# Token rows of 1024 columns with their halo tokens apart, V weights loaded behind the first freed block, and a first tile taken block by block, in an encoder block on eight cores

## The reference, cut to what matters

```python
p = x @ w_in                     # columns: [B_A | C_A | H_A | U_B | V_B | GATE_A | GATE_B]
gates = sigmoid(p[..., OFF_GA:] + b_gate)
a  = b_a * conv3_centred(c_a * h_a, conv_w)               # width 1536, depthwise over tokens
bb = gelu(u_b) * (W_s LN(gelu(v_b)) + b_s)                # per chunk of 128 tokens, 8 heads
mix = (g_a * (a @ w_pa) + g_b * (bb @ w_pb)) @ w_o
x1 = layernorm(ALPHA * x + mix, ln1_g, ln1_b)
out = layernorm(ALPHA * x1 + square(relu(x1 @ w_ff1)) @ w_ff2, ln2_g, ln2_b)
```

## Time and profile before

| | us |
|---|---|
| median of 3 runs | 1142.12 (1141.73 to 1142.21) |
| the profiled execution | 1143.57 |
| its span (slowest core, core 6) | 1141.9 |
| spans of all cores | 1135.9 to 1141.9 |
| PE busy | 1119.3 (98%) |
| DVE busy | 523.7 (46%) |
| ACT busy | 266.6 (23%) |
| POOL busy | 141.0 (12%) |

### The profile page before, as it was taken

One profiled execution on the slowest core, in us unless ns is written; L12 is line 12 of the kernel. 1 busy time (PEld: TensorE's weight loads), 2 busy tenths in 40 slices (PEclk: granted clock), 3 DMA queues, 4 the chain that ended last, 5 costly groups with the idle time before them and its releaser, 6 DMA issues.

```text
span 1141.9 us, 15721 instructions; the slowest of 8 cores (1135.9 to 1141.9 us)
## 1 busy us (share of the span) xinstructions
PE 1119.3 (98%) x5582; PEld 546.4 (48%) x5690; DVE 523.7 (46%) x750; ACT 266.6 (23%) x439; POOL 141.0 (12%) x257
## 2 busy tenths in 40 slices
PE   7989999999999999999999999999999999999997
PEld 3445555444444444444455555554444444444444
DVE  1835465322248434512467545642222763442356
ACT  1224323111114333100012343221111343330000
POOL 4302200000011010200120121000000101000000
PEclk9999999999999999999999999999999999999999
DMA  9986676355556674674367439555443717444412
GB/s 142 164 152 130 131 135 121 58 82 84 93 91 97 107 115 79 111 123 74 74 115 143 102 98 185 98 94 83 69 64 53 121 38 127 79 80 81 78 56 92
DMA packets 48219, 114.71 MB, mean 100 GB/s; under 512 B 20496, under 2 KB 20880, under 8 KB 47632
## 3 DMA queue, kind: packets, MB, share of 16 engines
q0 software_dynamic: 25056, 88.23, 47.9%
q1 hardware_dynamic: 23088, 25.48, 8.1%
HBM read 189.33 MB, written 8.39 MB: 173 GB/s over the span
## 4 chain that ended last, share of the span: by engine, by line
PE 93%; DMA 4%; POOL 1%; issue 1%; DVE 0%; ACT 0%; DVEq 0%; POOLq 0%; ACTq 0%
PE ps L264 93%; DMA ring<-wblk 2%; DMA regR<-xT 2%; POOL t L585 0%; POOL regR L150 0%; POOL ring L150 0%; ACT t L502 0%; DVE regQ L911 0%; DVE regQ L916 0%; DVE regQ L583 0%; DVEq L1007 0%; DVE st L930 0%; DVE regQ L928 0%; DVE st L932 0%; DVE t L588 0%
## 5 line engine op out<-in xcount | busy, mean ns | idle before, releaser
L264 PE MATMUL ps<-regR,ring 128*128 128x512 bf16 (+1 forms) x3267 | 651.1, 355 | 10.6 <-DMA regR<-xT 4.2
L264 PEld LDWEIGHTS ps<-regR,ring 128*128 128x128 bf16 x3328 | 318.9, 98 | 325.6 <-issue 15.1
L264 PE MATMUL ps<-ring,regP 128*128 128x512 bf16 (+1 forms) x1035 | 220.5, 372 | 1.5 <-DMA ring<-wblk 0.4
L150 POOL DMA_DIRECT2D ring<-wblk x144 | 77.1, 540 | 701.5 <-PE ps L264 696.7
L264 PEld LDWEIGHTS ps<-ring,regP 128*128 128x128 bf16 x1056 | 103.3, 98 | 118.7 <-issue 0.9
L264 PE MATMUL ps<-regP,ring 128*128 128x512 bf16 x628 | 143.1, 379 | 0.6
L878 DVE TENSOR_TENSOR regP<-t 128x512 bf16<-128x512 f32 x128 | 87.7, 692 | 116.5 <-ACT t L877 116.5
L755 DVE TENSOR_TENSOR t<-ps,t 128x512 f32<-128x512 f32 x64 | 44.1, 691 | 180.3 <-ACT t L753 180.0
L877 ACT ACTIVATE t<-ps 128x512 f32<-128x512 f32 x128 | 75.9, 597 | 136.0 <-PE ps L264 128.1
L264 PEld LDWEIGHTS ps<-regP,ring 128*128 128x128 bf16 x640 | 62.6, 98 | 75.5
L753 ACT ACTIVATE t<-ps,colv 128x512 f32<-128x512 f32 x64 | 43.8, 687 | 189.7 <-PE ps L264 189.7
(11 more groups left out here) (67 smaller groups left out, 483.9 us busy)
## 6 DMA issues: line engine op xcount, KB each, us to landing
ring<-wblk POOLq DMA_DIRECT2D x128, 512.0 KB, 7.6
bigW<-wbig POOLq DMA_DIRECT2D x4, 2048.0 KB, 21.8
regQ<-x SPq DMA_DIRECT2D x16, 512.0 KB, 5.6
y<-regQ SPq DMA_DIRECT2D x15, 512.0 KB, 2.6
ring<-wblk POOLq DMA_DIRECT2D x16, 384.0 KB, 8.7
regR<-xT POOLq DMA_DIRECT2D x16, 256.5 KB, 14.2
ring<-wfirst POOLq DMA_DIRECT2D x6, 256.0 KB, 16.0
t<-ln1g SPq DMA_DIRECT2D x2, 512.0 KB, 6.7
```

Of the source, the lines that this page charges most:

```text
L150: self.items.append(lambda e, out=out, in_=in_, sem=sem: e.dma_start(out=out, in_=in_, transpose=transpose).then_inc(sem, 16))
L264: return lambda e: e.matmul(out, lhsT=l, rhs=r, start=st, stop=sp_)
```

## The change

Three things are changed.

1. The token rows in HBM have 1024 columns instead of 1026. The halo tokens of both super-tiles come in a tensor of their own, `xhT` (128 x 32 float32, 16 columns for each super-tile), which SP loads once into `xhf` in the prologue. `place_halo` copies and casts a super-tile's 16 values per partition into columns 1024 and 1025 of `xT` on ACT: for the first super-tile in the prologue, for the second at the start of F2. A buffer record `xhB` makes the groups that read the halo wait for the copy.
2. `load_big(0)` and the load of `wsTb` leave the prologue for `load_v()`, called right behind `release(0)` in `first_groups`: on POOL they stand behind the issue of block 8 and ahead of those of blocks 9, 11 and 12.
3. In F2, the first tile of the part that goes tile by tile makes one group per block, instead of one group over all its blocks. This holds for every half; with lb = 7 it is seven groups.

```diff
-            DMA(pool, xT[:, k0:k0 + n, 0:TH], xT_d[r0:r0 + n * 128, :].rearrange("(p k) n -> p k n", k=n), xT_sem[c], writes=wr)
+            DMA(pool, xT[:, k0:k0 + n, 0:T], xT_d[r0:r0 + n * 128, :].rearrange("(p k) n -> p k n", k=n), xT_sem[c], writes=wr)
+
+        def place_halo(st):
+            OP(act, lambda e: e.activation(out=xT[:, :, T:TH], in_=xhf[:, st * 16:(st + 1) * 16].rearrange("p (k n) -> p k n", k=8), func=AF.Copy),
+               reads=[xhfB], writes=[xhB])
...
+            DMA(sp, xhf[:], xh_d, sem_xh, writes=[xhfB])
             DMA(sp, colv[:], cv_d, sem_cv, writes=[colvB])
+            place_halo(0)
...
             OP(pool, lambda e: e.memset(chalf[:, 1:2], LN_EPS), writes=[memB])
+
+        def load_v():
             load_big(0)
             DMA(pool, wsTb[:], wsT_d.rearrange("p (h i) -> p h i", h=8), sem_ws, writes=[wsTbB])
...
-                    PEG(fns, reads=deps_ + w0B[1] + xTB, writes=[bankB[gi], bankB[bx]])
+                    PEG(fns, reads=deps_ + w0B[1] + xTB + [xhB], writes=[bankB[gi], bankB[bx]])
...
                     for i in (0, 1, 3, 4):
                         release(i)
+                        if i == 0:
+                            load_v()
...
             if not last:
                 for c in range(len(PIECES)):
                     load_xT(st + 1, c)
+                place_halo(st + 1)
...
                 for tt in range(7 if split else 8):
-                    f2_part(st, h, tt, list(range(8 - lb, 8)))
+                    for qs in [[q] for q in range(8 - lb, 8)] if tt == 0 else [list(range(8 - lb, 8))]:
+                        f2_part(st, h, tt, qs)
                     f2_drain(tt, h, None, split)
...
-            rows.append(_pieces(np.concatenate([xpad[g0 + 1:g0 + T + 2], xpad[g0:g0 + 1]], axis=0).T, PIECES))
+            rows.append(_pieces(xpad[g0 + 1:g0 + T + 1].T, PIECES))
+            halos.append(np.stack([xpad[g0 + T + 1], xpad[g0]], axis=1).reshape(8, 128, 2).transpose(1, 0, 2).reshape(128, 16))
```

More of the change, by code:

```diff
@@ L155, in build_program @@
     x_d = nc.dram_tensor("x", [TOK, D], F32, kind="ExternalInput").ap()
-    xT_d = nc.dram_tensor("xT", [ST * 1024, TH], F32, kind="ExternalInput").ap()
+    xh_d = nc.dram_tensor("xhT", [128, ST * 16], F32, kind="ExternalInput").ap()
+    xT_d = nc.dram_tensor("xT", [ST * 1024, T], F32, kind="ExternalInput").ap()
     w0_d = nc.dram_tensor("wfirst", [2 * 1024, 512], F32, kind="ExternalInput").ap()
@@ L189, in build_program @@
         ones = sb("ones", [128, 128], F32)
+        xhf = sb("xhf", [128, ST * 16], F32)
         hy = sb("hy", [128, 4, 4], F32)
@@ L361, in build_program @@
         colvB = Buf(accum=True)
+        xhfB = Buf(accum=True)
+        xhB = Buf()
         wsTbB = Buf(accum=True)
@@ L367, in build_program @@
         bigW_sem = [semaphore("bigw"), 0]
+        sem_xh = [semaphore("ld_xh"), 0]
         sem_ws = [semaphore("ld_ws"), 0]
@@ L600, in first_groups @@
                 if n < 2:
-                    PEG(weave(fns, halos(n, 2 + n)), reads=[WBB] + w0B[0] + xTB, writes=[bankB[bbk], bankB[2 + n]])
+                    PEG(weave(fns, halos(n, 2 + n)), reads=[WBB, xhB] + w0B[0] + xTB, writes=[bankB[bbk], bankB[2 + n]])
                     halo_out(n, 2 + n, hcs[n])
@@ L663, in stage_A @@
                         PEG([mm(ps[:, b, 0:third], (LO if kc < 4 else HI)[:, kc % 4, cols], xT[:, kc, ts_], kc == 0, kc == 7) for kc in range(8)],
-                            reads=[LOB, HIB] + xTB, writes=[bankB[b]])
+                            reads=[LOB, HIB, xhB] + xTB, writes=[bankB[b]])
                     if j == 1 and i == 2:
@@ L1058, in _host_layout @@
         rows = []
+        halos = []
         for st in range(ST):
             g0 = c * TOK + st * T
-            rows.append(_pieces(np.concatenate([xpad[g0 + 1:g0 + T + 2], xpad[g0:g0 + 1]], axis=0).T, PIECES))
-        per_core.append((xc, np.concatenate(rows, axis=0)))
+            rows.append(_pieces(xpad[g0 + 1:g0 + T + 1].T, PIECES))
+            halos.append(np.stack([xpad[g0 + T + 1], xpad[g0]], axis=1).reshape(8, 128, 2).transpose(1, 0, 2).reshape(128, 16))
+        per_core.append((xc, np.concatenate(rows, axis=0), np.ascontiguousarray(np.concatenate(halos, axis=1))))
     return cvs, wsT, bsrow, per_core
@@ L1097 @@
         m["xT"] = per_core[c][1]
+        m["xhT"] = per_core[c][2]
         in_maps.append(m)
```

## The result

The changed kernel takes 1147.48 us (median of six runs) beside 1141.99 us before: ratio 1.0047, 95% interval 1.0035 to 1.0060. By the ratio it is slower by about 5.4 us, where -0.7 us was forecast; the time lies outside the stated range.

A forecast was written before the change was run, and what follows sets the result against it. TensorE bounds 93% of the span with untouched matmuls; only the DMA-full first 85 us and single waits could move. Core 5's 1139.3 + 3.0 - 0.8 - 1.8, plus 1.7 around the span, gave 1141.4 us, range 1138.8 to 1144.0.

The forecast's parts named there:

- The wait for block 8 goes, and one for block 10 takes its place at ca=6, behind a hole in the queue: Near 65 us PE's wait vanishes; near 84 us a weight-block wait of 2 to 3.5 us appears.
- The hole, 3.1 us on core 3 and 4.3 on core 5: DMA queue empty between the last prologue block's landing and block 8's: 3.1 us lost on core 3, 4.3 on core 5.
- All behind it later by the hole: Block 10 lands 3.1 us later on core 3 (87.3); PE's new waits are 2.2 and, on core 5, 3.45 us.
- The clock falls at the new wait: Rival at ca=6: price 1.5 us; 1142.9 with the rows' gain (chance 0.10), 1144.7 without (0.12).
- Token rows, -1.8: First set's eight token loads: rows of 1024 columns save half of 3.6 us, 1.8; second set worth nothing.
- Last half block by block, -0.8 on the slowest core: Wait in front of 1082.84 us for the last half's seventh block goes: -0.8 us on core 5, 0 on core 3.
- The sum for the slowest core: Core 5: 1139.3 + 3.0 - 0.8 = 1141.5, less 1.8 for the token rows gives 1139.7 us.

The follow-up runs named there:

- wsT late: Changed kernel with the wsT load issued behind block 10 instead of right behind the V weights: 1.0030 of before, 1144.94 us.
- a quarter of V: Changed kernel with two of eight channel blocks of the V weights loaded in the prologue, the rest and wsT behind block 8: 1.0008 of before.
- half did: Changed kernel with the first 1 MB of the V weights loaded in the prologue, the rest and wsT behind block 8: 0.9971 of before.
- the 28 matmuls: Changed kernel with 28 matmuls of 512 columns, result never read, put in front of ca=6: 1.0034 of before, 1145.86 us.

## Why the prediction was wrong

- **The wait for block 8 goes, and one for block 10 takes its place at ca=6, behind a hole in the queue.** Right, and the direction of the V edit with it: later on cores 3 and 5. The kernel with V moved alone shows that this edit costs 7.7 us.
- **The hole, 3.1 us on core 3 and 4.3 on core 5.** This is the step that failed. It put the end of the queue's work at the landing of the last prologue block. But most of the DMA engines were through earlier. On core 6 that block landed at 44.97 (12.1 + 32.9), while the DMA share was already 0.17 from 42 us on; a block's load has 16 records of 4 bytes near its end (block 8's lie between 51.7 and 53.1 us), and of the last 16 before the hole 13 lie between 41.2 and 42.0 us and three at 43.2, 43.4 and 44.4. The idle time is 4.3 to 6.9 us. The same reading made the queue full "to 84 us" in the kernel before: its share on core 3 is 0.60 and 0.32 ahead of block 10's landing at 84.2.

```profile
78.00:82.00 4.00, 4.00 (x23) 2.10 (x22) 2.07 (x4) 1.93 (x4) 1.01 (x3) 1.00 0.60 102
82.00:86.00 4.00, 4.00 (x21) 1.81 (x19) 3.75 (x4) 2.15 (x2) 1.14 (x2) 1.00 0.32 48
```

- **All behind it later by the hole.** It was more. Counted from the landing of the last prologue block, block 10 came 4.2 to 9.4 us later than on the same core before. Between the landings of blocks 8 and 10 stand the same bytes on every core, and they took 33.0 to 37.5 us. And block 8 itself took 5.0 to 5.2 us on four cores, as the late blocks of core 3 did, but 6.9 to 7.7 on the other four, among them the three that end last. Late blocks didn't stand for this place; why is open (last section). So the new wait is 6.5 to 7.6 us on the slowest three cores instead of 2.2 to 3.45. On core 5, whose 3.45 us the sum rests on, it was 3.56, and that is luck: 6.7 us idle instead of 4.3, made up by the bytes behind block 8, which took 33.0 us there. Cores 0, 2 and 6 had no such luck, and the forecast worked out the new wait for cores 3 and 5 alone and gave core 6 that of core 3.
- **The clock falls at the new wait.** The sum had it at nothing, though the 3.45 us of core 5 are more than the 2.98 at which core 6 had lost its clock; it was a rival, at 0.22 with and without the rows' gain. It fell on five of eight cores, at waits of 3.65 to 7.58 us, and held at 2.85, 3.41 and 3.56 us. The size of the wait alone doesn't settle it: with wsT late it fell at 3.54 us, with a quarter of V at 2.27 on core 5 and not at 2.24 on core 7, and core 6 before lost it at 2.98. The price was 1.5 us on core 6, as forecast, and up to 2.7 on core 2. The rival's times of 1142.9 and 1144.7 were too low because they took the forecast's wait.
- **Token rows, -1.8.** The number came out, -1.8 us alone, but by luck. Half of the second set's difference was taken, on the ground that the destination's step stays. With the destination unchanged the second set's step fell by 0.35 us on the mean of the cores, and on core 3 from 2.03 to 1.51, where weights take 1.58: the whole difference went, and the ground was wrong. The first set gained only 0.2 us per load (its eighth load lands at 27.6 instead of 29.2 us on the mean of the cores), and why less than the second is not shown.
- **Last half block by block, -0.8 on the slowest core.** The wait goes as said; with a wait on some cores alone the times don't resolve it. With V in the prologue it is at most the difference of 0.9984 and 0.9976, whose intervals overlap.
- **The sum for the slowest core.** Forecast, core 5 at 1139.7; measured, core 6 at 1146.0, which is 1105.2 + 31.63 + 7.58 + 1.5 by the table. Of the 6.3 us between them 4.1 are the wait (7.58 instead of 3.45) and 1.5 the clock; the rest is the start of the long row, 31.63 where core 5's 32.72 less 1.8 gives 30.9.

## What to carry to other kernels

A load that looks like an obstacle in a queue may be what fills it while the next one can't be issued yet. Before moving it, find what stands in the queue in its place, and take the end of the work from the DMA share, not from a landing; then move only as much as leaves the queue full (here half did; that it beats moving nothing is not shown). And when a wait is replaced by another, price the new one with the loads that surround it, and add what a fallen clock costs.

## What the hardware showed that was not expected

- **Rows of 2048 bytes instead of 2052 in SBUF (4096 instead of 4104 in HBM)** lower a load's step from 1.97 to 1.62 us, 18%, for 0.2% fewer bytes. By the Trainium skill (DMA: Bandwidth & Descriptors, How a descriptor splits into AXI transactions) the unaligned source would cost some 3%, an estimate from its rule; the trace shows six times that, and the tail of 4 bytes in SBUF (8 in HBM) and the alignment weren't tried apart.
- **Block 8 into an empty queue: 4.98 to 5.19 us on cores 1, 3, 4 and 7, 6.94 to 7.73 on cores 0, 2, 5 and 6.** One of each pair of neighbours is slow. The same is seen in the profiles of the other kernels in which block 8 meets idle engines (wsT late, the 28 matmuls, and cores 4 to 7 of V moved alone and of a quarter of V): of these 16 pairs, the changed kernel's four among them, 15 have one core at 4.9 to 5.4 us and one at 6.9 to 7.7, and in each of the 15 the slow one is the core that issued block 8 later after its own first instruction. In the 16th, cores 2 and 3 with wsT late, both are slow (6.76 and 6.53). The cause is open.
